# Local attention, rotation halves and the state space mixer's chunk products in half precision terms

## The reference, cut to what matters

```
proj = einsum('bsd,de->bse', h, w_in)          # 14 column groups
# state space mixer, chunks of 64 tokens, 16 heads of 64, state 128
y_intra = einsum('bcgjls,bcsgjp->bclgjp', cb[:, :, :, None] * decay, xdt)      # decay = exp(where(causal, cs_l - cs_s, -inf))
states  = einsum('bclgn,bclgj,bclgjp->bcgjpn', bm, decay_end, xdt)
y_inter = einsum('bclgn,bcgjpn,bclgj->bclgjp', cm, prev, exp(cs))
# local attention: 16 query heads, 4 key heads, window of two chunks, sinks
q, k = rope(q), rope(k)
sc = einsum('bclkrd,bcmkd->bckrlm', qc, kw) * 64 ** -0.5
m  = maximum(max(sc), sink); p = exp(sc - m); p = p / (sum(p) + exp(sink - m))
o  = einsum('bckrlm,bcmkd->bclkrd', p, vw)
# differential attention over all earlier chunks, also with rope; RG-LRU by a scan
yproj = einsum('bsnw,nwd->bsnd', ys, w_branch); out = einsum('bsd,de->bse', sum(gates * yproj), w_out)
```

## Time and profile before

| | us |
|---|---|
| median of 3 runs | 1915.69 (1913.7 to 1916.15) |
| the profiled execution | 1916.71 |
| its span, first to last instruction | 1914.8 |
| PE busy | 1890.6 (99%) |
| DVE busy | 1172.4 (61%) |
| ACT busy | 992.4 (52%) |
| POOL busy | 393.5 (21%) |

### The profile page before, as it was taken

How to read it: one execution, slowest core, us unless ns; L and a number is a source line. 1 busy time by engine, 2 the same in 40 slices (tenths; PEclk the granted TensorE clock), 3 DMA queues, 4 the chain that set the end, 5 groups by cost and what they waited for, 6 DMA issues and landing times.

```text
span 1914.8 us, 27900 instructions
## 1 busy us (share of the span) xinstructions
PE 1890.6 (99%) x11048; PEld 1020.4 (53%) x11048; DVE 1172.4 (61%) x1555; ACT 992.4 (52%) x1912; POOL 393.5 (21%) x266
## 2 busy tenths in 40 slices
PE   7999999999999999999999999999999999999998
PEld 4446765455455664544454477554554555655443
DVE  6677556587436777654367765655873468776432
ACT  5674454465334666543356645544662356765421
POOL 0212021142222332111001130112332222321110
PEclk9999999999999999999999999999999999999999
DMA  6224334443334655434222252354333344554421
GB/s 191 88 88 150 104 106 138 121 122 90 109 105 131 155 128 165 112 132 146 59 67 88 72 166 89 106 150 120 110 105 110 113 137 126 148 138 116 165 84 44
DMA packets 264747, 224.68 MB, mean 117 GB/s; under 512 B 88400, under 2 KB 253226, under 8 KB 264618
## 3 DMA queue, kind: packets, MB, share of 16 engines
q1 hardware_dynamic: 264618, 222.90, 39.3%
HBM read 182.96 MB, written 2.16 MB: 97 GB/s over the span
## 4 chain that ended last, share of the span: by engine, by line
PE 87%; DVE 4%; ACT 3%; issue 2%; POOL 2%; DMA 1%; SPq 1%; DVEq 0%; ACTq 0%; POOLq 0%
PE PS L591 85%; POOL X L1694 1%; DVE Y L1338 1%; DMA X<-X 1%; PE PS L695 1%; DVE X L1338 1%; ACT Y L1077 1%; DVE wsp L1335 1%; SPq L512 1%; DMA stage<-w_in 1%; ACT Y L1078 0%; SPq L564 0%; POOL Y L1694 0%; PE PS L819 0%; ACT wsp L1000 0%
## 5 line engine op out<-in xcount | busy, mean ns | idle before, releaser
L591 PE MATMUL PS<-hT,wsp 128*128 128x512 f16 (+2 forms) x4968 | 1083.2, 377 | 1.0 <-ACT hT L981 1.0
L591 PEld LDWEIGHTS PS<-hT,wsp 128*128 128x128 f16 x4968 | 479.5, 98 | 562.8 <-issue 13.6
L1335 DVE SCALAR_TENSOR_TENSOR wsp<-stage,wsp 128x2048 f16<-128x2048 f32 x148 | 352.9, 2384 | 164.8 <-ACT wsp L1000 162.6
L591 PE MATMUL PS<-ys,wsp 128*128 128x512 f16 x1536 | 339.4, 379 | 0.0
L1000 ACT ACTIVATE wsp<-stage 128x2048 f16<-128x2048 f32 x148 | 281.3, 1901 | 46.6 <-PE PS L591 44.7
L591 PEld LDWEIGHTS PS<-ys,wsp 128*128 128x128 f16 x1536 | 149.4, 98 | 178.4 <-issue 4.1
L591 PE MATMUL PS<-wsp,hT 128*128 128x256 f16 x1728 | 193.2, 273 | 0.0
L591 PEld LDWEIGHTS PS<-wsp,hT 128*128 128x128 f16 x1728 | 168.6, 98 | 22.7 <-issue 2.3
L1003 ACT ACTIVATE X<-PS 128x512 f32<-128x512 f32 (+1 forms) x120 | 68.4, 593 | 140.5 <-PE PS L591 108.2
L1694 POOL TENSOR_TENSOR X<-X,K 128x1024 f32<-128x1024 f32 x26 | 62.7, 2412 | 351.3 <-DMA X<-X 351.3
L1694 POOL TENSOR_TENSOR M<-M,T 128x512 f32<-128x512 f32 x48 | 67.4, 1407 | 292.1 <-DVE T L1335 292.1
(11 more groups left out here) (195 smaller groups left out, 1974.4 us busy)
## 6 DMA issues: line engine op xcount, KB each, us to landing
stage<-w_in SPq DMA_DIRECT2D x120, 1024.0 KB, 5.0
stage<-w_branch SPq DMA_DIRECT2D x32, 1024.0 KB, 5.3
X<-X SPq DMA_DIRECT2D x120, 128.0 KB, 2.4
stage<-w_out SPq DMA_DIRECT2D x8, 1024.0 KB, 5.4
Y<-sums SPq DMA_DIRECT2D x8, 512.0 KB, 6.3
M<-sums SPq DMA_DIRECT2D x8, 512.0 KB, 5.9
Y<-Y SPq DMA_DIRECT2D x24, 128.0 KB, 3.2
xres<-x SPq DMA_DIRECT2D x4, 512.0 KB, 6.7
```

The source lines that it names most:

```text
L591: return pe.matmul(o, a, b, start=start, stop=stop, skip_group_check=True)
L1335: return dve.scalar_tensor_tensor(out=o, in0=a, scalar=c, in1=b, op0=op0, op1=op1)
```

## The change

Five things. The state space mixer's est by xdt products become three f16 terms each (xdt is scaled by 64): ACT makes the hi halves (`chunk_hi`), DVE the lo halves (`chunk_lo`), and PE's step is 10. The exponential of a slot's decays moves from the slot's head into `falls` of the slot before, and `falls` moves ahead of `evacuate(p, 1)` on ACT. Local attention: both blocks of a slot are taken at once, the scaled exponentials are halved (`local_hi` on ACT, `local_lo` on DVE), one DMA transpose of 16 blocks of 128x128 (`turn_local`) takes the place of PE's transposes and ACT's copies, and `local_out` is three f16 terms. Rotation: ACT makes hi in one instruction of 128 rows, DVE (not POOL) makes lo in one, and all halves go to their places by DMA: 8 moves for kc and kd panels (4 before), 4 for qc and qd (2 before). `VALUES_AT` goes from 8 to 10, and the first `gates` waits for the read of the step sizes alone (`dt_taken`), not for all that is computed from them.

```diff
-VECTOR_FREES = {"vd", "xa", "conv", "ga", "z", "gc", "gd", "br", "out"}
+VECTOR_FREES = {"vc", "vd", "xa", "conv", "ga", "z", "gc", "gd", "br", "out"}
-VALUES_AT = 8
+VALUES_AT = 10
+X_SCALE = 64.0
@@ product_steps(p), for p in SSD_SLOT
-        return 11, 14
+        return 10, 14
@@ tiles
+ sH, sPT = (X[:, a:a + 1024].bitcast(F16).rearrange("p (h e n) -> p h e n", h=2, e=2) for a in (1024, 2048))
+ rhi, rlo = (T[:, a:a + 512].bitcast(F16).rearrange("p (u s) -> p u s", u=2) for a in (512, 0))
+ vC, vE = (Y[:, a:a + 1024].bitcast(F16).rearrange("p (h c n) -> p h c n", h=2, c=ST) for a in (2048, 7168))
+ est16 = ys[:, 1, 1024:2048].bitcast(F16).rearrange("p (h j l) -> p h j l", h=2, j=8)
+ xdt16 = ys[:, 1, 3072:3584].bitcast(F16).rearrange("p (h j n) -> p h j n", h=2, j=8)
@@ SyncE: a new function turn_local(k), called as turn_local(p - 2 - SWA0) after turn_differences, ahead of the swap
+ sp.wait_ge(s["sw_hi"], at("sw_hi", k + 1, layer))
+ sp.wait_ge(s["sw_lo"], at("sw_lo", k + 1, layer))
+ if k >= 1:
+     sp.wait_ge(s["sw_o"], at("sw_o", k, layer))
+ sp.dma_start_transpose(sPT.rearrange("p h e (g n) -> p (h e g) n", n=P), sH.rearrange("p h e n -> p (h e n)"))\
+     .then_inc(s["sw_turned"], 16)
@@ SyncE: moves of a rotated panel, for t in range(2)
-     if kind == "kc":
-         moves = ((kC[other, t], kC[own, t]), (kloC[other, t], kloC[own, t]))
-     elif kind == "kd":
-         moves = ((kD[i % 2][other, t], kD[i % 2][own, t]), (kloD[i % 2][other, t], kloD[i % 2][own, t]))
+     if kind in ("kc", "kd"):
+         hi, lo = (kC, kloC) if kind == "kc" else (kD[i % 2], kloD[i % 2])
+         moves = [(to[side, t], of[own]) for to, of in ((hi, rhi), (lo, rlo)) for side in (own, other)]
      else:
-         moves = (((qC if kind == "qc" else qD)[i % 2][other, t], by_chunks(kind, rlo[own])),)
+         to = (qC if kind == "qc" else qD)[i % 2]
+         moves = [(to[own, t], by_chunks(kind, rhi[own])), (to[other, t], by_chunks(kind, rlo[own]))]
@@ TensorE: before(p)
- if SWA0 < p <= SWA0 + 8:
-     for e in range(2):
...
-         for g in range(4):
-             last = pe.transpose(PS[:, 5 + 2 * e, P * g:P * g + P], sE[:, e, g, :], ident)
-         last.then_inc(s["sw_T"], 1)
@@ TensorE: between(p), for p in SSD_SLOT
- pe.wait_ge(s["ssd_mt"], at("ssd_mt", q + 1, layer))
+ pe.wait_ge(s["ssd_ml"], at("ssd_ml", q + 1, layer))
+ pe.wait_ge(s["ssd_xl"], at("ssd_xl", q + 1, layer))
+ for j in range(8):
+     o = PS[:, 4, HD * j:HD * j + HD]
+     mm(o, est16[:, 0, j, :], xdt16[:, 0, j, :], True, False)
+     mm(o, est16[:, 0, j, :], xdt16[:, 1, j, :], False, False)
+     last = mm(o, est16[:, 1, j, :], xdt16[:, 0, j, :], False, True)
  pe.wait_ge(s["ssd_x"], at("ssd_x", q + 1, layer))
- for j in range(8):
-     mm(PS[:, 4, HD * j:HD * j + HD], est[:, j, :], xdt[:, j, :], True, True)
@@ TensorE: local_out(p), for e in range(2)
- pe.wait_ge(s["sw_Ta"], at("sw_Ta", n + 1, layer))
+ if e == 0:
+     pe.wait_ge(s["sw_turned"], at("sw_turned", 16 * (n // 2 + 1), layer))
...
  for c in range(2):
-     keys = (vC if c else vE)[:, i, HD * j:HD * j + HD]
-     for t in range(2):
...
-         last = mm(o, keys, sPT[:, e, 2 * c:2 * c + 2, HD * t:HD * t + HD], True, True)
+     for k, (h, hp) in enumerate(((0, 0), (1, 0), (0, 1))):
+         keys = (vC if c else vE)[:, h, i, HD * j:HD * j + HD]
+         for t in range(2):
...
+             last = mm(o, keys, exps, k == 0, k == 2)
@@ TensorE: gates(p), at t == 0
- pe.wait_ge(s["dt_raw"], at("dt_raw", 1, layer))
- pe.wait_ge(s["dta_ready"], at("dta_ready", 1, layer))
+ pe.wait_ge(s["dt_taken"], at("dt_taken", 1, layer))
@@ ScalarE: decays(p) loses the exponential, falls(q) ends with it
- act.activation(est, seg[q % 2], ACT.Exp, scale=-1.0).then_inc(s["ssd_exp"], 1)
+ act.wait_ge(s["ssd_fall"], at("ssd_fall", q + 1, layer))
+ if q > 0:
+     act.wait_ge(s["ssd_ml"], at("ssd_ml", q, layer))
+ act.activation(est, seg[q % 2], ACT.Exp, scale=-1.0).then_inc(s["ssd_exp"], 1)
@@ ScalarE: chunk_hi(p), called after before(p); local_hi(p), called after differences_hi(p), ahead of evacuate(p, 0)
+ if q > 0:
+     act.wait_ge(s["ssd_out"], at("ssd_out", q, layer))
+ act.wait_ge(s["pool_chain"], at("pool_chain", q + 1, layer))
+ copy(xdt16[:, 0], xdt).then_inc(s["ssd_xh"], 1)
+ act.wait_ge(s["ssd_mt"], at("ssd_mt", q + 1, layer))
+ copy(est16[:, 0], est).then_inc(s["ssd_mh"], 1)
...
+ act.wait_ge(s["sw_n"], at("sw_n", k + 1, layer))
+ if k >= 1:
+     act.wait_ge(s["sw_turned"], at("sw_turned", 16 * k, layer))
+ copy(sH[:, 0], sE.rearrange("p e g n -> p e (g n)")).then_inc(s["sw_hi"], 1)
@@ ScalarE: rotated_hi(p)
- for t in range(2):
-     copy(dst[HD * t:HD * t + HD, t], by_chunks(kind, rcos[HD * t:HD * t + HD])).then_inc(s["rope_hi"], 1)
+ if n > 0:
+     act.wait_ge(s["rope_stack"], at("rope_stack", stacked_after(n - 1), layer))
+ copy(rhi, rcos).then_inc(s["rope_hi"], 1)
@@ ScalarE: the loop over slots
  middle(p)
+ if p + 1 == SSD_SLOT[0]:
+     falls(0)
+ if p in SSD_SLOT[:-1]:
+     falls(SSD_SLOT.index(p) + 1)
  if p > 0:
      evacuate(p, 1)
@@ VectorE: scores_in(p), for p in the local slots
+ link(dve.tensor_reduce(sm, PS[:, 4:6, :].rearrange("p e (g n) -> p e g n", g=4), AX, ALU.max, negate=True))
+ link(tt(m, m, sink, ALU.min))
+ tt(d, m, sink, ALU.subtract).then_inc(s["sw_m"], 1)
@@ VectorE: chunk_lo(p), local_lo(p), rotated_lo(p) (this one was GpSimd's)
+ dve.wait_ge(s["ssd_xh"], at("ssd_xh", q + 1, layer))
+ tt(xdt16[:, 1], xdt, xdt16[:, 0], ALU.subtract).then_inc(s["ssd_xl"], 1)
+ dve.wait_ge(s["ssd_mh"], at("ssd_mh", q + 1, layer))
+ tt(est16[:, 1], est, est16[:, 0], ALU.subtract).then_inc(s["ssd_ml"], 1)
...
+ dve.wait_ge(s["sw_hi"], at("sw_hi", p - SWA0 + 1, layer))
+ tt(sH[:, 1], sE.rearrange("p e g n -> p e (g n)"), sH[:, 0], ALU.subtract).then_inc(s["sw_lo"], 1)
...
+ tt(rlo, rcos, rhi, ALU.subtract).then_inc(s["rope_lo"], 1)
@@ VectorE: the loop over slots
+ chunk_lo(p)
  scans(p)
+ if SWA0 <= p < SWA0 + 8:
+     rotated(p)
+     for n in splits_in(p):
+         split_lo(n)
  before(p)
- if attention:
+ if DIFF0 <= p < DIFF0 + 16:
      rotated(p)
- local_gated(p)
- if attention:
      for n in splits_in(p):
          split_lo(n)
  differences_lo(p)
+ local_gated(p)
+ local_lo(p)
  evacuate(p, 0)
...
  middle(p)
+ rotated_lo(p)
  if p > 0:
      evacuate(p, 1)
@@ GpSimd: before xdt, between xdt and xw, between xw and yt (in this order now)
- pool.wait_ge(s["ssd_out"], at("ssd_out", q, layer))
- pool.wait_ge(s["ssd_y"], at("ssd_y", q, layer))
+ pool.wait_ge(s["ssd_xl"], at("ssd_xl", q, layer))
+ pool.wait_ge(s["ssd_x"], at("ssd_x", q, layer))
...
+ pool.wait_ge(s["ssd_out"], at("ssd_out", q, layer))
...
+ pool.wait_ge(s["ssd_y"], at("ssd_y", q, layer))
```

More of the change, by code:

```diff
@@ L107 @@
 LOCAL_OUT_AT = 8
+X_SCALE = 64.0
+LOCAL_SCORES = 2
 HEADS_AT = 6
@@ L328, in program @@
         eps64 = small[:, 108:109]
-        sinkP, nsp8 = small[:, 125:133], small[:, 133:141]
+        nsink, nsp8 = small[:, 125:133], small[:, 133:141]
         tapsA, tapsB = taps[:, 0:32], taps[:, 32:80]
@@ L541, in one_layer @@
                         kind, i = PANELS[p - 4][0:2]
-                        sp.wait_ge(s["rope_hi"], at("rope_hi", 2 * rope_index(p - 4) + 2, layer))
-                        sp.wait_ge(s["rope_lo"], at("rope_lo", 2 * rope_index(p - 4) + 2, layer))
+                        sp.wait_ge(s["rope_hi"], at("rope_hi", rope_index(p - 4) + 1, layer))
+                        sp.wait_ge(s["rope_lo"], at("rope_lo", rope_index(p - 4) + 1, layer))
+                        if kind == "qc" and i == 0:
+                            sp.wait_ge(s["ssd_out"], at("ssd_out", 8, layer))
@@ L551, in one_layer @@
                             for o, a in moves:
                                 sp.dma_start(o, a).then_inc(s["rope_stack"], 16)
+                    if p == SSD_SLOT[0]:
+                        sp.wait_ge(s["rope_stack"], at("rope_stack", stacked_after(0), layer))
+                        load_norm(0)
                     if DIFF0 <= p - 2 < DIFF0 + 16:
                         turn_differences(p - 2)
+                    if SWA0 <= p - 2 < SWA0 + 8:
+                        turn_local(p - 2 - SWA0)
@@ L704, in before @@
                                 pe.wait_ge(s["rope_stack"], at("rope_stack", stacked_after(1 + j), layer))
+                            if n >= 2 and e == 0:
+                                pe.wait_ge(s["sw_e"], at("sw_e", n // 2, layer))
                             own, prev, both = (slice(i * P, i * P + HD), slice(i * P - HD, i * P), slice(i * P, i * P + P))
@@ L1374, in evacuate @@
                         dve.wait_ge(s["dve_free"], at("dve_free", dve_frees(tile), layer))
-                    elif kind == "vd":
-                        dve.wait_ge(s["vd_hi"], at("vd_hi", 2 * i + u + 1, layer))
-                        hi, lo = (vD[i % 2][:, h, 2 * u:2 * u + 2, :].rearrange("p c n -> p (c n)") for h in range(2))
+                    elif kind in ("vc", "vd"):
```

(4 more changed lines are left out.)

242 lines of the change are left out of this document (111 added, 131 removed).

## The result

The changed kernel takes 1932.7 us (median of 5 runs, 1929.63 to 1938.52) against 1916.14 of the kernel before (1913.7 to 1916.55): slower by a ratio of 1.0094 (95% interval 1.0081 to 1.0107). Forecast were 1908.5, and 1924 as the end of the range. The profiled span grew from 1914.8 to 1931.2 us, 16.4 more, where 7.3 less had been forecast.

The account below looks back on a forecast made before the run. The prediction took PE, at work for 99% of the span, as the bound: 43.5 us off PE against 36.2 us of new waits gave −7.3 us, so a median of 1908.5 us, range 1884 to 1924.

Parts of the forecast that it names:

- PE's work: On PE: state space products save 16.5 us, dropped local transposes 13.9 us, local values 3.3 us.
- a sign of being wrong: The prediction's check on PE: its busy time falling by much other than 36 us would show it wrong.
- The first gates: PE's wait before the first gates goes, since they wait only for the first step-size instruction: 2.4 us saved.
- State space waits: New PE waits for est's lo half, 3.6 us in slot 18, 2.8 in slot 19; 15.3 us over both layers.
- The small ones: New state space waits of 0.3 us each in slots 20, 21, 23 and 25, 1.25 us a layer.
- Local waits: New PE waits for DMA transposes in slots 32, 34 and 36, 2.2 to 2.9 us each; 15.8 us over both layers.
- At nothing: Costs taken as zero: SP's added DMA issues, covered by the slot's 10 us, and POOL's, DVE's and ACT's changed work.
- the case without cover: If SP's added issues are not covered, the scores wait 1 to 2 us in up to eight slots.
- Differential waits: PE's waits for exponentials before values go, with values two steps later and the exponentials earlier: all 5.7 us.
- The clock: Of ten new PE waits of 2.2 to 3.6 us, three lose granted clock: 5.1 us, bounds 0 and 17.
- rival C: PE's clock falls after all ten new waits: +11.9 us, giving 1920 us; chance 0.10.

Follow-up runs that it names:

- e5: The changed kernel with qd and kd panels rotated as before (hi in place by ACT, lo by POOL, 2 and 4 moves): 1918.71 us.
- e4: The kernel before with only two of the edits, differential values at step 10 and the first gates waiting for the read of the step sizes alone: 1912.78 us.
- e11: e9 with the differential values at step 8 as in the kernel before: 1915.48 us.
- e10: e9 with local_out at step 13, local_lo ahead of local_gated, qc moves ahead of turn_local, and both rotation halves made earlier in local slots: 1905.03 us.
- e9: The changed kernel with qd and kd panels rotated as before and est by xdt at step 13 in slots 18 and 19: 1913.59 us.
- e3: The changed kernel with local_out at step 12, not 8, and DVE's local_lo ahead of its local_gated: 1930.1 us.
- e6: e3 with SP's moves of a qc panel one iteration earlier, ahead of turn_local: 1945.19 us.
- e12: The changed kernel with falls and its exponential behind evacuate(p, 1) on ACT, still in the slot ahead: 1983.89 us.

## Why the prediction was wrong, step by step

- *PE's work*: right. In a slot without waits PE gains 0.88 to 1.0 us in the state space part (forecast 1.03) and 1.11 in the local part (1.08). The 81 ns of the Trainium skill (TensorE: Matmul & The Clock Gate, section Back-to-back issue gap) are for 128 columns and did not appear: the 24 pairs of 64 columns in 0.71 us are 30 ns each, and pairs of 128 columns start 56 ns apart just ahead of slot 32's panel in both traces. PE's busy time fell by 20.1 us, not by 36, which the prediction had named as a sign of being wrong: the work fell by an estimated 33 (16 times 0.94 and 1.11), and 11.6 us more of half clock came back on it.
- *The first gates*: right, 2.6 us for 2.4.
- *State space waits*: right in place and size in slots 18 and 19 (3.6 and 2.8). The small ones were charged at 2.5 us in both layers and measured 1.7: 0.3 in slot 20 of both, 1.2 in slot 24 of one.
- *Local waits*: right. Six of 2.2 to 3.3, in all 15.5 us, for 15.8. Missed were two waits for qc moves, 1.1 us, by the same mechanism as the next.
- *"At nothing": SP's issues.* **This is the step that failed.** I gave SP the slot's 10 us and said that the halves are needed "a slot or more later". But a kd panel is moved in the slot ahead of its scores, with 0.5 to 2.4 us to spare (0.6 in slot 52). What had to be added was four issues of 0.62 us and a start that is up to 1.1 us later: the last move is issued 2.2 to 3.9 us later. The landing, 4.0 to 6.3 us with a panel load in flight, was nearly as long before (4.2 to 6.2). It cost 9.7 of the 10.8 us of waits for moves, in six slots (my own price for the case without cover, "1 to 2 us in up to eight slots", would have given it); e5, which takes it away, has the differential slots at 0.9 in place of 11.5. DVE, in the same paragraph, rose by 23.8 us, not 82.
- *Differential waits*: **failed too**, by some 5 us. 4.3 of 5.7 us stay, and e4 and e11 show that a later step gains next to nothing: where it takes these waits off, others (DVE's evacuation, the moves of kd halves) stand in their place.
- *The clock*: three of ten waits was too few, and rival C was nearer. It cost 13.5 us, 1.9 before: 11.6 more, where 3.4 was in the sum. Right was that it is a term of its own: e10, with the same work as e9 and shorter waits, has 0.999.

Laid out: moves 10.8, values 5 and clock 8.2 are 24.0, and the forecast was off by 16.4 + 7.3 = 23.7. That the three come so close is partly chance, as the terms for values and clock are not measured apart from each other. No rival had SP's queue in it.

## What to carry to other kernels

An edit that adds DMAs is priced at the latest use of what they carry, from the start of their issue on the queue, not at the queue's free time: here 0.5 to 2.4 us of slack stood against 2.2 to 3.9 us of later issue. How long they take to land is read where they will stand in the queue, and not from a median over the kernel: 5.7 us with a panel load in flight, 2.4 without. When a wait is worth a step or two, move the producer (e10's lo half in a gap of DVE) before moving the consumer; a later consumer alone showed the next late thing (e3, e4), and an order that waits earlier on one queue moved the loss to what is behind it (e6). An instruction put behind an engine's wait for the end of a panel begins in the next slot, whatever slot it was written in (e12).

## What was not expected of the hardware

- A single wait of 2.1 us left the clock at 1.00 (405 to 415), and waits of 2.8 and 3.6 us were followed by windows at 0.83; which wait is followed by 1.2 GHz was not the same in the two layers, with the same waits in both (0.97 and 0.93 over 50 us). The changed kernel's five runs lie 8.9 us apart, at granted clocks of 0.992 to 0.994; the clock accounts for some 4 us of that, as an estimate from these means.
- The four moves of a qc panel behind a transpose of 16 blocks and a panel load were slow to issue: 5.61 us in e3 and 5.51 in the changed kernel, and 2.85 ahead of both in e6 and e10. In these slots one of the four took 2.5 to 3.4 us, and its issue ended within 0.5 us of the landing of the load. Which of the two ahead of them it is was not tested.
- A move of 128 KB lands in 2.2 to 6.4 us in the changed kernel, and how many go out together doesn't decide it: eight in slot 48 land in 2.2 to 2.4 us, four in slot 50 in 5.8 to 6.1. The first had no panel load in flight, the second one issued 0.7 us ahead.
